# Folding four-by-four block weights into gate and key matrices: TensorE transposes and matmuls, or elementwise products on VectorE

## The chip, the cores and the metric

The kernel runs on one core of a Trainium2 chip. The metric is the device time of one execution in microseconds (us), lower is better. The core has TensorE (PE, matmuls, with its weight loads shown as PEld), VectorE (DVE), ScalarE (ACT), GpSimd (POOL), and SyncE (SP), which issues most DMAs.

## What is computed

The reference runs two transformer-like blocks on one sequence of 1024 positions and 1024 features. The change touches the mLSTM branch of the first block, cut here to what matters:

```python
QKV_BLOCK = 4          # w_q, w_k, w_v: (256, 4, 4); D_MLSTM = 1024
def headwise(u, w):    # block-diagonal linear map
    return jnp.einsum('bsni,nio->bsno', u.reshape(B, S, w.shape[0], w.shape[1]), w).reshape(B, S, -1)
...
    c = jax.nn.silu(centred_depthwise_conv(u, conv_w, conv_b))
    q = headwise(c, w_q)
    k = headwise(c, w_k)
    v = headwise(u, w_v)
    qkv = jnp.concatenate([q, k, v], axis=-1).astype(jnp.float32)
    gates = jnp.einsum('bsc,ncg->nbsg', qkv, w_gates.astype(jnp.float32)) \
        + b_gates.astype(jnp.float32)[:, None, None, :]
```

The kernel does not form q, k and v for the gates. It folds each block-diagonal map into the gate weights: gates = c (Wq Gq + Wk Gk) + u (Wv Gv), where G is `w_gates` (2 directions, 3072 rows, 8 columns). For the attention-like scores q k it folds likewise: with A = Wk Wq^T / 16 it needs only c and c A.

## The kernel before

Everything is fp32. A large projection is done as three matmuls of 512 columns on split operands (high and low parts, tiles `whi`, `wlo` of the weights and `u_hi`, `u_lo` of the activations; lines 829 to 831). A "group" is 24 such matmuls (8 pieces of the contraction times 3) into one PSUM bank, or 12 for the output projections. Weights come in chunks of 1 MB: SyncE loads chunk w into `wraw` once chunk w-1 has been split (`wt`, lines 391 and 394), and GpSimd splits it (`split`: a cast to `whi`, L610, a subtraction to `wlo`, L612).

The stages around the change, in the order in which TensorE meets them:

1. Output projection of the pool branch: chunks `W_OP` to `W_OP + 3`, eight 12-matmul groups each, in quarters q = 0 to 3. For each group VectorE adds the PSUM bank to `hst` (L1418), 32 additions in all. Quarters 0 and 1 fill one half of the features, 2 and 3 the other. Quarter 0 uses eight banks, the later ones take turns on four. SyncE loads `hst` (L453), stores finished parts (`hpool`, L457) and reloads, in an order written out by hand.
2. Projection `W_MX` to `W_MX + 3`, four groups each. ScalarE copies each group to `um` (L2020). VectorE runs the five-tap convolution over `um`, eight tiles `cva` (L1429, L1433), ScalarE's silu writes `cc` (L2008).
3. After each of the chunks `W_MX + 1` to `W_MX + 3`: GpSimd has expanded one of w_q, w_k, w_v (tile `wn`) to eight block-diagonal 128x128 tiles `bd` (L638), TensorE transposes the eight (L956), ScalarE copies them to `bt` (L2013).
4. Projection `W_MZ` to `W_MZ + 3`, four groups each; ScalarE writes `mzs` (L2036). After the second group of `W_MZ` TensorE multiplies `bt` by the gate weights `wg` (L967 for q and k, L970 for v; 16 columns each) and `bt` by `bt` (L976, eight of 128 columns). ScalarE copies the results to `ga` (L2040) and `Amat` (L2044).
5. After the fourth group of `W_MZ`: the gate sums, 32 matmuls of `ga` with `cc` and `um` (L986), then a reduction (L995), and from there a chain of row operations that ends before the recurrent units start. Heads 0 to 3 follow, with `Amat` applied in `headwise` (L1026).

The places that a sentence can't say:

```python
            for n in range(3):
                for i in range(4):
                    group(W_MX + n + 1, i, u_hi, u_lo, "a_um", 4 * n + 4 + i + 1)
                for b in range(2):
                    ps = ring_x("a_bt", 2 * n + b + 1)
                    for i in range(4):
                        pe.wait_ge(s["g_bd"], KT * n + 4 * b + i + 1)
                        mm = pe.transpose(ps[:, i * P:(i + 1) * P], bd[:, 4 * b + i, :], idn)
```

## Time and profile before

| what | value |
|---|---|
| median of 3 timed runs | 1254.55 us (1253.87 to 1254.64) |
| the profiled execution's own time | 1250.48 us |
| its span, first to last instruction | 1248.6 us |
| PE / PEld / DVE / ACT / POOL busy | 1208.9 / 966.7 / 660.4 / 349.6 / 469.4 us |
| mean granted TensorE clock | 0.990 of full speed |

The span is what the trace covers; times in the rows are us from its start. Busy time is the union of an engine's instructions. The trace was taken in one execution, whose own time is 4.07 us under the median of the timed runs. DMA queue rows (SPq) show the issue of a transfer, not its flight.

### The profile page before, as it was taken

Reading aid. Unit: us, or ns where it says so; the run is one execution under the profiler, and the core shown is the slowest. Engines: PE = TensorE matmul, PEld = TensorE weight load, DVE = VectorE, ACT = ScalarE, POOL = GpSimd, SP = SyncE. Lnnn points to the kernel's source line nnn. Section 1 sums busy time; section 2 is a strip of 40 time slices with the busy share of each in tenths; the row PEclk is TensorE's granted clock in tenths of the full one; section 3 lists DMA queues with packets and bytes.
Section 4 is the critical chain, followed back from the end, with each engine's and each line's share of the span. In section 5 each row is a group of like instructions: output and inputs, shape, how many; then the busy total and the mean of one; then the engine's idle time right before and its main releaser. Section 6 shows DMA issues by size and latency. Waiting matters only on the chain.

```text
span 1248.6 us, 15984 instructions
## 1 busy us (share of the span) xinstructions
PE 1208.9 (97%) x5977; PEld 966.7 (77%) x5977; DVE 660.4 (53%) x1220; ACT 349.6 (28%) x710; POOL 469.4 (38%) x449
## 2 busy tenths in 40 slices
PE   6999999999999999999998999889999999999995
PEld 5777878788888878787786788779888886667784
DVE  4325355422465203167767946856694525445468
ACT  6211110100022112446565421321111144433211
POOL 3224222232545223444665654314322324443343
PEclk9999999999999999999999999989999999999998
DMA  6131121243311223100114412222121110051112
GB/s 216 56 131 43 36 75 34 101 169 101 75 49 53 68 68 106 60 26 24 54 39 144 166 46 70 83 97 69 51 68 35 59 35 35 5 190 34 37 50 118
DMA packets 72702, 92.84 MB, mean 74 GB/s; under 512 B 12721, under 2 KB 51849, under 8 KB 72114
## 3 DMA queue, kind: packets, MB, share of 16 engines
q1 hardware_dynamic: 63906, 87.62, 21.0%
q10 hardware_dynamic: 8720, 4.20, 1.2%
q8 instruction: 49, 0.80, 0.3%
q14 instruction: 27, 0.22, 0.1%
HBM read 74.45 MB, written 18.92 MB: 75 GB/s over the span
## 4 chain that ended last, share of the span: by engine, by line
PE 88%; DVE 6%; POOL 2%; DMA 1%; issue 1%; ACT 1%; SPq 0%; ACTq 0%; POOLq 0%; DVEq 0%
PE bank L829 22%; PE bank L831 21%; PE bank L830 21%; PE bank L1078 3%; PE bank L1095 3%; PE wide L1251 2%; PE wide L930 2%; PE bank L1232 2%; PE wide L1241 2%; PE wide L1088 2%; DVE res L1908 1%; DMA wraw<-in_w_in 1%; PE bank L1038 1%; PE bank L1049 1%; PE bank L1026 1%
## 5 line engine op out<-in xcount | busy, mean ns | idle before, releaser
L610 POOL CAST whi<-wraw 128x2048 fp32r<-128x2048 f32 x32 | 60.6, 1894 | 448.9 <-PE bank L831 361.1
L829 PE MATMUL bank<-u_hi,wlo 128*128 128x512 f32 x512 | 202.7, 396 | 2.9 <-DVE u_lo L1349 2.9
L831 PE MATMUL bank<-u_hi,whi 128*128 128x512 f32 x512 | 200.1, 391 | 0.0
L830 PE MATMUL bank<-u_lo,whi 128*128 128x512 f32 x512 | 199.9, 390 | 0.0
L612 POOL TENSOR_TENSOR wlo<-wraw,whi 128x2048 fp32r<-128x2048 f32 x33 | 155.9, 4725 | 3.1 <-ACT whi L2230 0.5
L829 PE MATMUL bank<-x_hi,wlo 128*128 128x512 f32 x320 | 129.2, 404 | 7.2 <-POOL wlo L612 6.4
L830 PE MATMUL bank<-x_lo,whi 128*128 128x512 f32 x320 | 125.5, 392 | 0.0
L831 PE MATMUL bank<-x_hi,whi 128*128 128x512 f32 x320 | 125.5, 392 | 0.0
L829 PEld LDWEIGHTS bank<-u_hi,wlo 128*128 128x128 f32 x512 | 96.6, 189 | 25.9 <-DVE u_lo L1349 4.0
L831 PEld LDWEIGHTS bank<-u_hi,whi 128*128 128x128 f32 x512 | 96.5, 188 | 20.4
L830 PEld LDWEIGHTS bank<-u_lo,whi 128*128 128x128 f32 x512 | 96.5, 188 | 20.2 <-issue 0.7
L829 PEld LDWEIGHTS bank<-x_hi,wlo 128*128 128x128 f32 x320 | 60.6, 189 | 28.8 <-issue 9.8
L775 POOL TENSOR_SCALAR sp<-sp,rcx 128x384 f32<-128x384 f32 (+1 forms) x64 | 36.0, 575 | 112.3 <-DVE rcx L1840 112.3
L831 PEld LDWEIGHTS bank<-x_hi,whi 128*128 128x128 f32 x320 | 60.6, 189 | 13.1
L830 PEld LDWEIGHTS bank<-x_lo,whi 128*128 128x128 f32 x320 | 60.7, 190 | 11.6
L1753 DVE SCALAR_TENSOR_TENSOR wide<-glu,VT,wide 128x1024 f32<-128x1024 f32 x58 | 69.3, 1283 | 0.0
L1095 PE MATMUL bank<-v,kwb 128*128 128x257 f32 x224 | 58.2, 383 | 1.1 <-DVE Cst L1556 0.9
L1078 PE MATMUL bank<-Cst,qT 128*128 128x257 f32 x224 | 58.1, 381 | 0.9 <-ACT tmpj L2149 0.8
L2020 ACT ACTIVATE um<-bank 128x512 f32<-128x512 f32 x16 | 9.6, 599 | 157.2 <-PE bank L831 157.2
L698 POOL TENSOR_TENSOR Pm<-ST,Wb 128x128 f32<-128x128 f32 x64 | 30.4, 475 | 59.0 <-ACT Wb L2101 59.0
L829 PE MATMUL bank<-whi,ym_lo 128*128 128x512 f32 x128 | 50.2, 392 | 0.2 <-ACT tmpj L2149 0.2
L1834 DVE CUSTOM_DVE_ANT_0 sp<-bank,rbias,nsink 128x384 f32<-128x384 f32 (+1 forms) x64 | 34.9, 583 | 29.4 <-PE bank L1232 29.1
(330 smaller groups left out, 2430.7 us busy)
## 6 DMA issues: line engine op xcount, KB each, us to landing
wraw<-in_w_in SPq DMA_DIRECT2D x27, 1024.0 KB, 5.4
wraw<-in_w_out SPq DMA_DIRECT2D x12, 1024.0 KB, 5.1
xr<-in_x SPq DMA_DIRECT2D x8, 512.0 KB, 8.7
hst<-in_x SPq DMA_DIRECT2D x4, 1024.0 KB, 6.0
hpool<-hst SPq DMA_DIRECT2D x4, 1024.0 KB, 4.1
smz<-mzs SPq DMA_DIRECT2D x16, 256.0 KB, 2.1
wraw<-nmax ACTq DMA_DIRECT2D x32, 128.0 KB, 3.0
h<-hpool SPq DMA_DIRECT2D x4, 1024.0 KB, 6.8
```

What stands on the lines that cost most here:

```text
L610: g_.tensor_copy(whi[w % 2][:, :, :], wraw[:, :, :]).then_inc(s["w_hi"], 1)
L612: g_.tensor_tensor(wlo[w % 2][:, :, :], wraw[:, :, :], whi[w % 2][:, :, :].bitcast(F32), ALU.subtract).then_inc(s["w_lo"], 1)
L698: g_.tensor_tensor(Pm[:, n % 2, :], STs[h % 2][:, ck, :], Wb[:, n % 2, :], ALU.mult).then_inc(s["g_P"], 1)
L775: g_.tensor_scalar(row, row, rcx[:, x % 2, i:i + 1], 0.5 if g else 1.0, ALU.mult, ALU.mult).then_inc(s["g_nm"], 1)
L829: pe.matmul(ps, al, bh, start=(k == 0), stop=False)
L830: pe.matmul(ps, ah, bl, start=False, stop=False)
L831: return pe.matmul(ps, ah, bh, start=False, stop=(k == nk - 1))
L930: mm = pe.matmul(ps[:, :], pw[:, g % 2, k, dt * P:(dt + 1) * P], px[:, k, PAD + nh * HALF:PAD + (nh + 1) * HALF], start=(k == 0), stop=(k ...
L1078: mm = pe.matmul(ps[:, 0:AUG], q[:, k, ck * P:(ck + 1) * P], Cst[:, d, k, :], start=(k == 0), stop=(k == 1))
L1095: mm = pe.matmul(ps[:, 0:AUG], kwb[:, m % 2, k * P:(k + 1) * P], v[:, ck, :], start=True, stop=True)
L1753: ins = ve.scalar_tensor_tensor(dst, src, w, acc, ALU.mult, ALU.add)
L1834: ve.tensor_tensor_reduce(sp[:, x % 2, i, BAND - nb * P:BAND], ps[:, 0:nb * P], rbias[:, 2 * p + i, off:off + nb * P], 1.0, nsink[:, h:h + 1],
```

## The change

The products with the four-by-four blocks are no longer made on TensorE. The gate weights are loaded in another arrangement, four neighbouring rows of `w_gates` per partition, the same in four partitions (`wgx`, partitions i, i+4, ...; eight DMAs of 32 partitions), and so is `w_k` (`wkx`, four DMAs). VectorE then multiplies `wgx` by `wn`, with each of its four columns spread over eight gates (two products of 128x768), sums over the four (two reductions), and adds the q and k parts or copies the v part straight into `ga`; `fold_keys` makes the four-by-four blocks of A (`ak`) in the same way, and GpSimd expands `ak` to `Amat`. These eight steps stand on VectorE one ahead of each addition of quarter 2 of the pool output projection. The DMAs stand on SyncE right behind the load of `W_OP + 2`. The 24 transposes, the 32 small matmuls, `bd`, `bt`, `wg` and the nine ScalarE copies go. The gate sums wait for `v_ga` and `g_init`; the first use of `Amat` waits for `g_am`. The ring of banks 4 to 7 (`ring_x`) is taken nine times fewer, so later takers get another bank than before.

The core of the diff (names of tiles and semaphores left out):

```diff
@@ -227,7 +227,7 @@
-         cva, mzs, bd, bt, wg, ga,
+         cva, mzs, _m, wgx, gx, gr, ga, wkx, kx, ak,
-            [("cva", [P, 2, S], F32), ("mzs", [P, 2, HALF], F32), ("bd", [P, KT, P], F32),
-             ("bt", [P, 3, KT, P], F32), ("wg", [P, 24, 2, 8], F32), ("ga", [P, 16, 32], F32)],
+            [("cva", [P, 2, S], F32), ("mzs", [P, 2, HALF], F32), ("_m", [P, KT, P], F32),
+             ("wgx", [P, 2, 24, 4, 8], F32), ("gx", [P, 2, 24, 4, 8], F32), ("gr", [P, 2, 24, 8], F32),
+             ("ga", [P, 16, 32], F32), ("wkx", [P, KT, 4, 4], F32), ("kx", [P, KT, 4, 4], F32),
+             ("ak", [P, KT, 4], F32)],
...
@@ -459,6 +461,13 @@
             for q in range(2):
                 load_h(0, q)
             wt(W_OP + 2)
+            for i in range(4):
+                for d in range(2):
+                    sp_.dma_start(wgx[i::4, d, :, :, :],
+                                  I["w_gates"][0, d].rearrange("(c b o) g -> b c o g", b=32, o=4)
+                                  ).then_inc(s["l_wg"], 16)
+                sp_.dma_start(wkx[i::4, :, :, :], I["w_k"][0].rearrange("(j b) i o -> b j i o", b=32)
+                              ).then_inc(s["l_wg"], 16)
             for q in range(2):
                 store_h(0, q)
                 sp_.wait_ge(s[f"o_h{q}"], 16)
@@ -469,9 +478,6 @@
                 store_h(1, q)
             for q in range(2):
                 sp_.wait_ge(s[f"o_h{q}"], 32)
-            for d in range(2):
-                sp_.dma_start(wg[:, :, d, :], I["w_gates"][0, d].rearrange("(c p) g -> p c g", p=P)
-                              ).then_inc(s["l_wg"], 16)
             for w in range(W_OP + 6, W_MZ + 2):
                 wt(w)
 
@@ -629,20 +635,20 @@
 
             g_.wait_ge(s["l_wn"], 48)
             g_.wait_ge(s["l_cst"], 16)
+            g_.wait_ge(s["v_ylo"], 16)
+            g_.memset(ga[:, :, 16:32], 0.0).then_inc(s["g_init"], 1)
+            g_.wait_ge(s["v_ga"], 7)
             g_.wait_ge(s["o_h0"], 32)
             g_.wait_ge(s["o_h1"], 32)
-            g_.memset(ga[:, :, 16:32], 0.0).then_inc(s["g_init"], 1)
             blk = cst[:, C_BLK:C_BLK + 32].unsqueeze(2).to_broadcast([P, 32, 4])
 
-            def expand(dst, n, j):
+            def expand(dst, four):
                 return g_.tensor_tensor(dst.rearrange("p (b o) -> p b o", o=4),
-                                        wn[:, n, j, :].unsqueeze(1).to_broadcast([P, 32, 4]), blk, ALU.mult)
-
+                                        four.unsqueeze(1).to_broadcast([P, 32, 4]), blk, ALU.mult)
+
+            for j in range(KT):
+                expand(Amat[:, j, :], ak[:, j, :]).then_inc(s["g_am"], 1)
             for n in range(3):
-                if n:
-                    g_.wait_ge(s["t_bt"], 2 * n)
-                for j in range(KT):
-                    expand(bd[:, j, :], n, j).then_inc(s["g_bd"], 1)
                 split(W_MX + 2 + n)
...
-                    expand(bdh[:, m, :], 2, 2 * h + m).then_inc(s["g_bdh"], 1)
+                    expand(bdh[:, m, :], wn[:, 2, 2 * h + m, :]).then_inc(s["g_bdh"], 1)
...
@@ -949,47 +955,23 @@
             for n in range(3):
                 for i in range(4):
                     group(W_MX + n + 1, i, u_hi, u_lo, "a_um", 4 * n + 4 + i + 1)
-                for b in range(2):
-                    ps = ring_x("a_bt", 2 * n + b + 1)
-                    for i in range(4):
-                        pe.wait_ge(s["g_bd"], KT * n + 4 * b + i + 1)
-                        mm = pe.transpose(ps[:, i * P:(i + 1) * P], bd[:, 4 * b + i, :], idn)
-                    mm.then_inc(s["t_bt"], 1)
-
             for i in range(4):
                 group(W_MZ, i, u_hi, u_lo, "a_mz", i + 1)
-                if i == 1:
-                    pe.wait_ge(s["a_bt"], 6)
-                    pe.wait_ge(s["l_wg"], 32)
-                    ps = ring_x("a_bt", 7)
-                    for j in range(KT):
-                        for n in range(2):
-                            pe.matmul(ps[:, j * 16:j * 16 + 16], bt[:, n, j, :], wg[:, KT * n + j, :, :],
-                                      start=(n == 0), stop=(n == 1))
-                    for j in range(KT):
-                        mm = pe.matmul(ps[:, (KT + j) * 16:(KT + j) * 16 + 16], bt[:, 2, j, :],
-                                       wg[:, 2 * KT + j, :, :], start=True, stop=True)
-                    mm.then_inc(s["t_bt"], 1)
-                    for b in range(2):
-                        ps = ring_x("a_bt", 8 + b)
-                        for k in range(4):
-                            mm = pe.matmul(ps[:, k * P:(k + 1) * P], bt[:, 0, 4 * b + k, :], bt[:, 1, 4 * b + k, :],
-                                           start=True, stop=True)
-                        mm.then_inc(s["t_bt"], 1)
-            pe.wait_ge(s["a_bt"], 7)
+            pe.wait_ge(s["v_ga"], 6)
+            pe.wait_ge(s["g_init"], 6)
             pe.wait_ge(s["a_c"], KT)
             for nh in range(2):
-                ps = ring_x("a_bt", 10 + nh)
+                ps = ring_x("a_gsum", nh + 1)
                 for j in range(16):
                     q = 32 * (j % 4)
                     src = cc if j < KT else um
                     mm = pe.matmul(ps[q:q + 32, :], ga[:, j, :], src[:, j % KT, nh * HALF:(nh + 1) * HALF],
                                    start=(j < 4), stop=(j >= 12))
-                mm.then_inc(s["t_bt"], 1)
+                mm.then_inc(s["t_gsum"], 1)
             for i in range(4):
                 group(W_MZ + 1, i, u_hi, u_lo, "a_mz", 4 + i + 1)
                 if i == 1:
-                    pe.wait_ge(s["a_bt"], 11)
+                    pe.wait_ge(s["a_gsum"], 2)
                     ps = ring_x("v_gs", 4)
                     for t in range(NT):
                         mm = pe.matmul(ps[:, t * 16:t * 16 + 16], gsum[:, t * P:(t + 1) * P],
@@ -1022,6 +1004,8 @@
                 n, i = i // 4, i % 4
                 if n == 0:
                     m, nh = i // 2, i % 2
+                    if h == 0 and i == 0:
+                        pe.wait_ge(s["g_am"], KT)
                     ps = fill("a_hq", 12 * h + i + 1)
                     mm = pe.matmul(ps[:, :], Amat[:, 2 * h + m, :], cc[:, 2 * h + m, nh * HALF:(nh + 1) * HALF],
                                    start=True, stop=True)
@@ -1407,9 +1391,45 @@
                                          ).then_inc(s["v_ylo"], 1)
                         ve.wait_ge(s["v_ylo"], n + 1)
 
+            def fold_gates(step):
+
+                if step < 2:
+                    if step == 0:
+                        ve.wait_ge(s["l_wn"], 48)
+                        ve.wait_ge(s["l_wg"], 16 * 12)
+                    w = wn[:, :, :, :].rearrange("p n j o -> p (n j o)").unsqueeze(2).to_broadcast([P, 96, 8])
+                    ins = ve.tensor_tensor(gx[:, step, :, :, :].rearrange("p c o g -> p (c o) g"),
+                                           wgx[:, step, :, :, :].rearrange("p c o g -> p (c o) g"), w, ALU.mult)
+                elif step < 4:
+                    ve.wait_ge(s["v_ga"], step - 1)
+                    ins = ve.tensor_reduce(gr[:, step - 2, :, :],
+                                           gx[:, step - 2, :, :, :].rearrange("p c o g -> p c g o"), AX_X, ALU.add)
+                elif step == 4:
+                    ve.wait_ge(s["v_ga"], 4)
+                    ins = ve.tensor_tensor(ga[:, 0:KT, 0:16].rearrange("p j (d g) -> p d j g", d=2),
+                                           gr[:, :, 0:KT, :], gr[:, :, KT:2 * KT, :], ALU.add)
+                else:
+                    ins = ve.tensor_copy(ga[:, KT:2 * KT, 0:16].rearrange("p j (d g) -> p d j g", d=2),
+                                         gr[:, :, 2 * KT:3 * KT, :])
+                ins.then_inc(s["v_ga"], 1)
+
+            def fold_keys(step):
+
+                if step == 0:
+                    wq = wn[:, 0, :, :].unsqueeze(2).to_broadcast([P, KT, 4, 4])
+                    chain(ve.tensor_tensor(kx[:, :, :, :], wkx[:, :, :, :], wq, ALU.mult))
+                else:
+                    chain(ve.tensor_reduce(ak[:, :, :], kx[:, :, :, :], AX_X, ALU.add))
+                    ve.tensor_scalar(ak[:, :, :], ak[:, :, :], HD ** -0.5, None, ALU.mult).then_inc(s["v_ga"], 1)
+
             for q in range(4):
                 for t in range(NT):
                     n = 8 * q + t
+                    if q == 2:
+                        if t < 6:
+                            fold_gates(t)
+                        else:
+                            fold_keys(t - 6)
                     if q % 2:
                         ve.wait_ge(s["v_hp"], n - 7)
                     else:
@@ -2007,12 +2027,6 @@
                 ac.wait_ge(s["v_conv"], j + 1)
                 ac.activation(cc[:, j, :], cva[:, j % 2, :], ACT.Silu).then_inc(s["a_c"], 1)
 
-            def bt_copy(n):
-                for b in range(2):
-                    ps = filled(ac, "t_bt", 2 * n + b + 1, "a_bt", 2 * n + b + 1)
-                    ac.activation(bt[:, n, 4 * b:4 * b + 4, :], ps[:, :].rearrange("p (j c) -> p j c", j=4), ACT.Copy
-                                  ).then_inc(s["a_bt"], 1)
-
             for h in range(NH):
                 for i in range(4):
                     m, nh = i // 2, i % 2
@@ -2023,8 +2037,6 @@
                         conv_silu(2 * h - 2)
                     if h and i == 3:
                         conv_silu(2 * h - 1)
-                if h:
-                    bt_copy(h - 1)
             conv_silu(6)
             for n in range(16):
                 h, m, nh = n // 4, n % 4 // 2, n % 2
@@ -2034,19 +2046,10 @@
                 if n >= 2:
                     ac.wait_ge(s[f"o_mz{n % 2}"], 16 * (n // 2))
                 ac.activation(mzs[:, n % 2, :], ps[:, :], ACT.Silu).then_inc(s["a_mz"], 1)
-                if n == 1:
-                    ps = filled(ac, "t_bt", 7, "a_bt", 7)
-                    ac.wait_ge(s["g_init"], 6)
-                    ac.activation(ga[:, :, 0:16], ps[:, 0:2 * P].rearrange("p (j g) -> p j g", j=16), ACT.Copy
-                                  ).then_inc(s["a_bt"], 1)
-                    for b in range(2):
-                        ps = filled(ac, "t_bt", 8 + b, "a_bt", 8 + b)
-                        ac.activation(Amat[:, 4 * b:4 * b + 4, :], ps[:, :].rearrange("p (j c) -> p j c", j=4),
-                                      ACT.Copy, scale=HD ** -0.5).then_inc(s["a_bt"], 1)
                 if n == 3:
                     for nh in range(2):
-                        ps = filled(ac, "t_bt", 10 + nh, "a_bt", 10 + nh)
-                        ac.activation(gsum[:, nh * HALF:(nh + 1) * HALF], ps[:, :], ACT.Copy).then_inc(s["a_bt"], 1)
+                        ps = filled(ac, "t_gsum", nh + 1, "a_gsum", nh + 1)
+                        ac.activation(gsum[:, nh * HALF:(nh + 1) * HALF], ps[:, :], ACT.Copy).then_inc(s["a_gsum"], 1)
                 if n == 9:
 
                     ac.wait_ge(s["v_rif"], 2)
```

Where the instructions stand, engine by engine. Operand names are tiles of the program (`wide` and `bank` are PSUM), "waits" lists semaphores, xN is N alike in a row. TensorE before, after the second group of `W_MZ`:

```order
L831 MATMUL bank<-u_hi,whi 128x512
L967 MATMUL wide<-wg,bt 128x16 [waits a_bt,l_wg]
L967 MATMUL wide<-wg,bt 128x16 x15
L970 MATMUL wide<-wg,bt 128x16 x8
L976 MATMUL wide<-bt 128x128 [waits a_bt]
L976 MATMUL wide<-bt 128x128 x3
L829 MATMUL bank<-u_hi,wlo 128x512 [waits a_um,w_lo]
```

TensorE now, from the end of the fourth group of `W_MZ` (the second group runs straight into the third):

```order
L837 MATMUL bank<-u_hi,whi 128x512
L968 MATMUL wide<-cc,ga 32x512 [waits a_c,v_hp,g_init,v_ga]
L968 MATMUL wide<-cc,ga 32x512 x7
L968 MATMUL wide<-um,ga 32x512 x8
L968 MATMUL wide<-cc,ga 32x512 [waits v_hp]
L835 MATMUL bank<-u_hi,wlo 128x512 [waits a_mz,w_lo]
```

The small matmuls are gone, and the gate sums (L986 before) are now L968, the first that waits for the fold. SyncE now, from the load of `W_OP + 2`:

```order
L393 DMA wraw<-in_w_out 128x4x512 [waits w_lo]
L466 DMA wgx<-in_w_gates 32x24x32 x2
L469 DMA wkx<-in_w_k 32x8x16
...
L459 DMA hpool<-hst 128x4x512 [waits v_hp]
L455 DMA hst<-in_x 128x4x512 [waits o_h0]
L393 DMA wraw<-in_w_out 128x4x512 [waits w_lo]
```

The three lines L466, L466, L469 come four times, twelve DMAs, where there was none between `wraw` and `hpool`; the two of `wg` that stood before the load of `W_OP + 6` are gone. VectorE now, from the first addition of quarter 2:

```order
L1438 TENSOR_TENSOR hst<-bank,hst 128x512 [waits t_gemm,v_hp] x8
L1401 TENSOR_TENSOR gx<-wgx,wn 128x768 [waits l_wg,l_wn]
L1438 TENSOR_TENSOR hst<-bank,hst 128x512 [waits t_gemm,l_xh0]
L1401 TENSOR_TENSOR gx<-wgx,wn 128x768
L1438 TENSOR_TENSOR hst<-bank,hst 128x512 [waits t_gemm,l_xh0]
L1405 TENSOR_REDUCE gr<-gx 128x192 [waits v_ga]
...
L1409 TENSOR_TENSOR ga<-gr 128x2x8x8 [waits v_ga]
...
L1422 TENSOR_REDUCE ak<-kx 128x32
L1423 TENSOR_SCALAR ak<-ak 128x32 [waits v_chain]
```

Before, these were additions alone (L1418); each now has one or two small instructions ahead of it.

## Rows read from the trace of the kernel before

**Rows 1.** The page's first part: engine, busy us, share of the span, instructions.

```profile
PE 1208.9 (97%) x5977; PEld 966.7 (77%) x5977; DVE 660.4 (53%) x1220; ACT 349.6 (28%) x710; POOL 469.4 (38%) x449
```

**Rows 2.** The page's chain that ended last, by engine.

```profile
PE 88%; DVE 6%; POOL 2%; DMA 1%; issue 1%; ACT 1%; SPq 0%; ACTq 0%; POOLq 0%; DVEq 0%
```

**Rows 3.** Timeline of ACT: start us, us, line, operation, idle before and its releaser.

```profile
356.89 0.60 ACT L2020 ACTIVATE um<-bank 128x512 f32<-128x512 f32 x1 [4.85 <-PE bank L831]
363.25 0.60 ACT L2020 ACTIVATE um<-bank 128x512 f32<-128x512 f32 x1 [3.84 <-PE bank L831]
...
402.26 0.60 ACT L2020 ACTIVATE um<-bank 128x512 f32<-128x512 f32 x1 [4.85 <-PE bank L831]
...
408.62 0.60 ACT L2036 ACTIVATE mzs<-bank 128x512 f32<-128x512 f32 x1 [2.89 <-PE bank L831]
414.36 1.06 ACT L2008 ACTIVATE cc<-cva 128x1024 f32<-128x1024 f32 x1 [5.14 <-DVE cva L1433]
...
428.30 0.60 ACT L2036 ACTIVATE mzs<-bank 128x512 f32<-128x512 f32 x1 [4.87 <-PE bank L831]
433.74 0.60 ACT L2036 ACTIVATE mzs<-bank 128x512 f32<-128x512 f32 x1 [4.84 <-PE bank L831]
```

**Rows 4.** Windows: stretch, length, then busy us of each engine, granted clock, DMA share, GB/s.

```profile
413.80:419.00 5.20, 5.20 (x48) 5.16 (x48) 0.52 (x1) 1.54 (x2) 0.00 (x0) 1.00 0.24 86
419.00:422.50 3.50, 3.50 (x20) 3.50 (x19) 0.00 (x0) 0.98 (x2) 0.00 (x0) 0.53 0.00 0
...
433.60:440.60 7.00, 7.00 (x65) 1.98 (x64) 0.00 (x0) 1.19 (x2) 6.45 (x2) 1.00 0.10 37
```

**Rows 5.** Groups of PE instructions in 413.8 to 422.6: busy us, mean ns, idle before.

```profile
L976 PE MATMUL wide<-bt 128*128 128x128 f32 x16 | 3.7, 423 | 0.0
L967 PE MATMUL wide<-wg,bt 128*128 128x16 f32 x32 | 3.6, 260 | 0.0
L970 PE MATMUL wide<-wg,bt 128*128 128x16 f32 x16 | 1.9, 263 | 0.0
```

**Rows 6.** Timeline of DVE, the additions at the start of quarter 2.

```profile
272.63 0.69 DVE L1418 TENSOR_TENSOR hst<-bank,hst 128x512 f32<-128x512 f32 x1 [2.03 <-PE bank L831]
275.35 0.69 DVE L1418 TENSOR_TENSOR hst<-bank,hst 128x512 f32<-128x512 f32 x1 [2.03 <-PE bank L831]
```

**Rows 7.** Timeline of SP, issues of DMAs during stage 1.

```profile
231.16 0.51 SPq L391 DMA_DIRECT2D wraw<-in_w_out  x1
259.75 0.37 SPq L457 DMA_DIRECT2D hpool<-hst  x1
263.91 0.37 SPq L453 DMA_DIRECT2D hst<-in_x  x1
264.32 1.27 SPq L391 DMA_DIRECT2D wraw<-in_w_out  x1
```

**Rows 8.** Lines 424 and 473 on SP: issue ns min/median/max, first and last start us; landing.

```profile
L424 SPq DMA_DIRECT2D wn<-in_w_k x1: 2645/2645/2645, 14.2 to 14.2; - x1
...
L473 SPq DMA_DIRECT2D wg<-in_w_gates x2: 373/1558/2742, 318.4 to 318.8; - x2
...
DMA to landing us min/median/max: 4.0/5.0/6.1
```

**Rows 9.** Timeline of POOL: the splits in stage 1 and at 337 us.

```profile
273.31 1.90 POOL L610 CAST whi<-wraw 128x2048 fp32r<-128x2048 f32 x1 [18.55 <-DMA wraw<-in_w_out]
275.29 4.62 POOL L612 TENSOR_TENSOR wlo<-wraw,whi 128x2048 fp32r<-128x2048 f32 x1
...
337.19 4.93 POOL L612 TENSOR_TENSOR wlo<-wraw,whi 128x2048 fp32r<-128x2048 f32 x1
```

**Rows 10.** Timeline of DVE, convolution: one instruction, and four of the next tile.

```profile
337.70 5.50 DVE L1433 SCALAR_TENSOR_TENSOR cva<-um,VT,cva 128x1022 f32<-128x1022 f32 x1
...
348.50 5.24 DVE L1433 SCALAR_TENSOR_TENSOR cva<-um,VT,cva 128x1022 f32<-128x1022 f32 x4
```

**Rows 11.** Windows, as Rows 4: a stretch with TensorE idle.

```profile
810.00:820.00 10.00, 6.03 (x17) 4.80 (x18) 9.74 (x11) 1.49 (x2) 5.06 (x4) 0.66 0.13 52
```

8 lines of the change are left out of this document (4 added, 4 removed).

## The prediction

> **What bounds the kernel now.** I read the page first. TensorE is busy for 1208.9 of the 1248.6 us of the span [rows 1], and the chain of waits that ended last lies on TensorE for 88% [rows 2]. So an instruction taken off TensorE shortens the run by its own time, unless TensorE then waits for something else. An instruction added to VectorE (busy for 53%) costs nothing as long as it fits into that engine's gaps. The rest of the reading answers two questions: how long the removed TensorE work takes, and whether each thing that TensorE will now wait for is ready in time.
>
> For the first I went to ScalarE's timeline, not to the matmul durations: matmuls overlap, but ScalarE takes each group's bank as soon as the group ends, so the distances between its copies are the true pace of TensorE [rows 3]. A group without extras takes 5.44 us (428.30 to 433.74).
>
> **What goes from TensorE.** One block of eight transposes lies between the copies at 356.89 and 363.25: 6.36 us in place of 5.44, so 0.92 us [rows 3]. The third block reads the same (402.26 to 408.62, 6.36). Three blocks: **2.75 us**. The small matmuls (L967, L970, L976) stand behind the second group of `W_MZ`. Its own copy was held up on ScalarE by the silu at 414.36, so I count from the first group's copy: 408.62 to the third group's at 428.30 is 19.68 us for two groups (10.88) and the block. The block costs **8.80 us** [rows 3]. The instructions' own times agree: 3.6, 1.9 and 3.7 us [rows 5]. Sum: **11.55 us**, and nothing is added to TensorE, only waits.
>
> **The clock inside that block.** TensorE had no idle time from 413.80 to 419.00, at full clock (2.4 GHz), yet from 419.00 to 422.50 the granted clock is 0.53, that is nearly all at the lower level, 1.2 GHz [rows 4]. Work of 16-column matmuls came before the fall. Of the 8.80 us, 3.50 x (1 - 0.53) = 1.6 us are this slow stretch, and they leave with the block. The Trainium skill ("TensorE: Matmul & The Clock Gate", "What's actually happening") says that the half rate is the default and comes back after idleness. That rule and the row disagree here: the engine was busy all through. By the rule alone the block would have run at full clock, and the sum would be 1.6 us less; the trace has the fall, so I keep 8.80.
>
> **What is added to SyncE and the DMA queues.** Twelve DMAs are issued behind the load at 231.16 (issued by 231.67), and the next one in the old order is the store at 259.75 [rows 7]: 28.1 us of room. No row shows a DMA of this shape. The nearest are the gate weights' and key weights' own loads, many small pieces too: 0.37 to 2.74 us to issue, landing in 4.0 to 6.1 us [rows 8]. Twelve issues take 4.4 us at the lower end. At the upper end, 32.9 us, SyncE is free at 264.6, so 4.8 us late for the store. I take the middle of the range, 12 x 1.56 = 18.7 us, since it comes from the load of the same tensor, and it costs nothing. At the upper end the store, the reload at 263.91 and the weight load at 264.32 all slip by 4.8 us. The additions of quarter 2 start at 272.63 and today wait for TensorE, not for the reload [rows 6], so they slip by 4.8 us at most. GpSimd's split of the late chunk (273.31 to 279.91 [rows 9]) would end at 284.7. TensorE needs it for the first group of quarter 3. Additions come every 2.72 us [rows 6], so that group starts 7 x 2.72 = 19.0 us after 272.63, at 291.7. Hidden. The two `wg` issues that go had their own room and are worth nothing.
>
> **What is added to VectorE.** An addition of 512 columns takes 0.69 us and is followed by 2.03 us of waiting for TensorE [rows 6]. By columns a fold product of 768 takes 1.04 us; I give each of the two reductions the same, with twice that as the upper bound since it reads with a stride. The five small instructions are under 0.69 us each. That is at most 4 x 1.04 + 5 x 0.69 = 7.6 us in eight gaps that hold 16.2. What if one is late? TensorE has four banks, so an addition may slip by three groups less its own time, 8.16 - 0.69 = **7.5 us**, before TensorE stalls. There is one hazard. A convolution step issued at 337.70 took 5.50 us where four together take 5.24, and ended a microsecond after GpSimd's subtraction of 337.19 to 342.12 [rows 9, 10]: both read two tensors in SBUF. The second fold product comes at 273.3, in the middle of a split. If it waits for its end at 279.91, the next addition starts at 281.0 and not 275.35, 5.6 us late, still inside 7.5. Cost: nothing. The Trainium skill ("SBUF — State Buffer", "SBUF: two separate sides") speaks against such a placing: VectorE instructions with two SBUF inputs and GpSimd hold a shared port pair for a whole instruction, and the other blocks. The rows agree (5.50 us against 1.31). If every two-input fold met a full subtraction, lateness would add up past the slack; that is in the second rival.
>
> **What moves elsewhere.** GpSimd has 16 fewer expansions and no wait for TensorE's transposes, and its eight `Amat` expansions stand where eight `bd` ones stood. ScalarE loses nine copies. None was what TensorE waited for: nothing. The gate sums now stand 11.55 us earlier, at 422.1 in place of 433.6 [rows 4], and wait for the last silu. It ended at 414.36 + 1.06 = 415.4 [rows 3]. Even if it did not move, 6.7 us are left, and one more blocked convolution step (5.50 - 1.31 = 4.2 us) fits into that. Everything behind (row operations, heads, the second block) is released by TensorE's results and moves along.
>
> **The sum.** The profiled execution took 1250.48 us and should take 1238.9 (span 1237.1). The timed median is 1254.55, 4.07 above it; the same 11.55 us gives **1243.0 us**. A measurement of this kernel tells about 0.2%, 2.5 us, from no change.
>
> **The rivals.**
> - *The clock falls elsewhere* (chance 0.08). The fall follows the work around it and may reappear beside the gate sums, or in a stretch where TensorE idles, as at 810 to 820 with 0.66 [rows 11]. For it: matmuls run almost without a pause into the gate sums. Against: in 433.60 to 440.60 they ran at a granted clock of 1.00 [rows 4], and they are 512 columns wide. Price: one such stretch, 1.6 us, up to two: 1244.6 to 1246.2. The Trainium skill ("TensorE: Matmul & The Clock Gate", same section) calls the monitor free-running, so such falls need not stay with a place.
> - *VectorE's cover breaks* (0.07). Slow issues make the additions 4.8 us late; the second product is then issued at 278.1 beside a split of 278.1 to 284.7 and ends at 285.7, 10.4 us late. TensorE stalls for 10.4 - 7.5 = 2.9 us: 1245.9. Against: it needs both upper ends.
> - *Slower: the twelve copies land one behind the other* (0.04). The first product waits for all twelve, and every addition queues behind it. At 6.1 us each they are in at 231.7 + 73.2 = 304.9; with the product the addition starts at 305.9, 33.3 us late, TensorE stalls for 25.8, net +14.3: 1268.8. It decides from 4.9 us per copy (lateness 19.05 = 7.5 + 11.55). Against: today's loads overlap, and two of 96 KB each landed in 4.0 and 6.1 us [rows 8].
> - *The gate sums wait for the convolution* (0.02): two more blocked steps, 8.4 us against 6.7, and partly given back: 1244.7.
> - *No change* (0.03): the 11.55 us come back as waits of TensorE in the later stages that VectorE and GpSimd share in the chain (8% [rows 2]). For it: that share. Against: they start from TensorE's output and move along. 1254.5.
>
> **How the numbers follow.** The forecast has 0.76, and its own range is 1241 to 1245 (two microseconds either way for pauses that shift in later stages and for the spread of the runs). The clock and the broken cover take the range up to 1247; downward 1240.3, if the clock also loses less in a later idle stretch. The slower case and no change stay outside. Faster by over 0.2%: 0.76 + 0.08 + 0.07 + 0.02 = 0.93; within: 0.03; slower: 0.04.
>
> **What would show it.** Right: ScalarE's copies at 5.44 us from group to group from the first of `W_MX` to the fourth of `W_MZ`; the gate sums near 422 with no idle time before them; the granted clock 1.00 there; the small VectorE instructions at about 1 us in the gaps of quarter 2, the additions every 2.72 us; the store at 259.75 unmoved; the stretch from the gate sums to the end as long as before. Wrong: TensorE idle between 275 and 300 with VectorE as releaser, a row of `gx` released by a DMA, an idle time before the gate sums, or a later stage that has grown by microseconds.

## The result and the profile after

| | before | after |
|---|---|---|
| median of the timed runs, same chip | 1254.21 us (4 runs, 1252.36 to 1254.64) | 1239.2 us (4 runs, 1237.97 to 1240.01) |
| ratio, with 95% interval | | 0.9882 [0.9865, 0.9899] |
| profiled execution, own time | 1250.48 us | 1238.44 us |
| its span | 1248.6 us | 1236.4 us |
| mean granted clock | 0.990 | 0.992 |

The change is faster, by 1.2%. The forecast was 1243.0 us with a range of 1240.3 to 1247.0. The time lies 1.1 us below that range. The gain was 15.0 us (the ratio gives 14.8), against 11.55 forecast. Between the two *profiled* executions it is 12.04 us: 1238.44 us was measured where the sum gave 1238.9. So the sum nearly holds for the profiled pair and not for the timed medians. That is the hint: something differed between the profiled execution of before and the ones that were timed. One of the 91 executions of the kernel before in all comparisons took 1528.84 us at a granted clock of 0.751, and it is left out everywhere below.

The page's first part after the change, to be held against [rows 1]:

```profile
PE 1196.0 (97%) x5889; PEld 953.8 (77%) x5889; DVE 673.2 (54%) x1229; ACT 345.2 (28%) x701; POOL 456.5 (37%) x433
```

TensorE has 88 instructions and 12.9 us less, and is as full as before. VectorE has nine more (a net 12.8 us, of which the fold's own are 6.8; most of the rest is in the convolution, see below), ScalarE nine fewer (the copies), GpSimd sixteen fewer (the expansions).

ScalarE's timeline, the copies that pace TensorE, to be held against [rows 3]:

```profile
360.40 0.60 ACT L2034 ACTIVATE um<-bank 128x512 f32<-128x512 f32 x1 [3.89 <-PE bank L837]
365.84 0.60 ACT L2034 ACTIVATE um<-bank 128x512 f32<-128x512 f32 x1 [4.84 <-PE bank L837]
...
403.92 0.60 ACT L2048 ACTIVATE mzs<-bank 128x512 f32<-128x512 f32 x1 [2.95 <-PE bank L837]
410.55 1.06 ACT L2028 ACTIVATE cc<-cva 128x1024 f32<-128x1024 f32 x1 [6.04 <-DVE cva L1453]
...
414.80 0.60 ACT L2048 ACTIVATE mzs<-bank 128x512 f32<-128x512 f32 x1 [2.70 <-PE bank L837]
420.24 0.60 ACT L2048 ACTIVATE mzs<-bank 128x512 f32<-128x512 f32 x1 [4.84 <-PE bank L837]
```

Every distance is now 5.44 us: 360.40 to 365.84, and 403.92 to 414.80 is two groups, 10.88. The transposes and the small matmuls have left without a trace, and 428.30 has become 414.80. The last silu ends at 410.55 + 1.06 = 411.6.

TensorE's timeline at the gate sums, and below it the windows of that stretch (columns as in [rows 4]):

```profile
419.81 0.39 PE L837 MATMUL bank<-u_hi,whi 128*128 128x512 f32 x1
420.13 1.92 PE L968 MATMUL wide<-cc,ga 128*32 128x512 f32 x16
```

```profile
413.80:419.00 5.20, 5.20 (x25) 4.30 (x24) 0.00 (x0) 0.60 (x1) 0.00 (x0) 1.00 0.13 50
...
420.20:427.20 7.00, 7.00 (x65) 1.97 (x65) 0.00 (x0) 1.20 (x2) 6.46 (x2) 1.00 0.11 40
```

No idle time stands before the gate sums, at 420.1 us, and the clock is 1.00 all through. They have 420.1 - 411.6 = 8.5 us in hand against the silu that they wait for.

VectorE's timeline of the convolution shows one more thing that moved. One tile (four steps), before and after:

```profile
359.51 5.32 DVE L1433 SCALAR_TENSOR_TENSOR cva<-um,VT,cva 128x1022 f32<-128x1022 f32 x4
```

```profile
357.54 9.46 DVE L1453 SCALAR_TENSOR_TENSOR cva<-um,VT,cva 128x1022 f32<-128x1022 f32 x4
```

Before, two of the eight tiles held a step of 5.50 us beside a GpSimd subtraction; now four do. These are the two more blocked steps that the prediction's fourth rival asks for, 8.4 us in sum. They fell into different tiles, in time that VectorE had to spare, and cost nothing: the last tile, with one blocked step, is as it was. The count is four in every trace with the fold, also where TensorE's work was put back (both_back below), so it goes with what changed on GpSimd and VectorE and not with TensorE's pace.

VectorE's timeline in quarter 2, where the fold stands in the gaps of [rows 6]:

```profile
267.99 0.69 DVE L1438 TENSOR_TENSOR hst<-bank,hst 128x512 f32<-128x512 f32 x1 [2.03 <-PE bank L837]
268.60 0.95 DVE L1401 TENSOR_TENSOR gx<-wgx,wn 128x768 f32<-128x768 f32 x1
270.71 0.69 DVE L1438 TENSOR_TENSOR hst<-bank,hst 128x512 f32<-128x512 f32 x1 [1.16 <-PE bank L837]
271.32 1.43 DVE L1401 TENSOR_TENSOR gx<-wgx,wn 128x768 f32<-128x768 f32 x1
273.43 0.69 DVE L1438 TENSOR_TENSOR hst<-bank,hst 128x512 f32<-128x512 f32 x1 [0.68 <-PE bank L837]
274.04 1.59 DVE L1405 TENSOR_REDUCE gr<-gx 128x192 f32<-128x768 f32 x1
276.15 0.69 DVE L1438 TENSOR_TENSOR hst<-bank,hst 128x512 f32<-128x512 f32 x1 [0.52 <-PE bank L837]
```

The additions still come every 2.72 us and still wait for TensorE; only their idle time has shrunk, from 2.03 to 0.52 us at the least. That is how a hidden cost looks. The fold of the keys behind them is small (0.28, 0.28 and 0.18 us). The hazard of the prediction, a product held up to the end of a split, did not come: the second product ran into a GpSimd cast (270.04 to 271.94) and took 1.43 us in place of 0.95, and both reductions took 1.59 us beside the subtraction that started at 272.01.

SyncE's timeline, to be held against [rows 7]:

```profile
229.79 3.97 SPq L466 DMA_DIRECT2D wgx<-in_w_gates  x2
...
243.89 0.65 SPq L469 DMA_DIRECT2D wkx<-in_w_k  x1
257.83 0.38 SPq L459 DMA_DIRECT2D hpool<-hst  x1
```

The twelve issues run from 229.79 to 244.5 and the store still stands 1.9 us ahead of 259.75, the shift that the whole trace has there: SyncE had been idle for 13 us. Nothing landed later than 9.5 us after its issue, and so at least 15 us before the product at 268.60.

Laid on top of each other, instruction by instruction, the two traces differ by -1.9 us from the first 20 us on (start-up, granted clock 0.66 in 15 to 20 us before, 1.00 after), three times -0.9 at the transposes, -8.8 at the block, +1.9 at the first unit of the recurrence, and -0.6 at a stall near 810 us: -12.2. So the sum of 11.55 us is there to a tenth, and two other things of 1.9 us each cancelled, which is luck. The start-up goes with the execution and not with the kernel: a second trace of the changed kernel (after_again) has 0.69 in 15 to 20 us, and from there on stands 1.4 us behind the first. The loss at the first unit does go with the kernel. It is the prediction's first rival, "The clock falls elsewhere", which had a chance of 0.08 and a price of 1.6 us.

### The profile page after: what moved, and what is told of

Its sections match the earlier page's. It is cut to its first block, busy times and chain, and to the rows that moved or that the text cites. A ratio compares the mean times of both kernels' runs of the same rounds, so it can differ in the third digit from the quotient of the medians.

```text
span 1236.4 us, 15797 instructions
## 1 busy us (share of the span) xinstructions
PE 1196.0 (97%) x5889; PEld 953.8 (77%) x5889; DVE 673.2 (54%) x1229; ACT 345.2 (28%) x701; POOL 456.5 (37%) x433
## 4 chain that ended last, share of the span: by engine, by line
PE 87%; DVE 6%; POOL 2%; DMA 1%; issue 1%; ACT 1%; SPq 0%; ACTq 0%; POOLq 0%; DVEq 0%
PE bank L835 22%; PE bank L837 21%; PE bank L836 21%; PE bank L1062 3%; PE bank L1079 3%; PE wide L1235 2%; PE wide L936 2%; PE bank L1216 2%; PE wide L1225 2%; PE wide L1072 2%; DVE res L1928 1%; DMA wraw<-in_w_in 1%; PE bank L1022 1%; PE bank L1033 1%; PE bank L1010 1%
## 5 line engine op out<-in xcount | busy, mean ns | idle before, releaser
L1453 DVE SCALAR_TENSOR_TENSOR cva<-um,VT,cva 128x1022 f32<-128x1022 f32 (+1 forms) x32 | 58.0, 1811 | 1.1
```

The source lines that it names most:

```text
L1453: ins = ve.scalar_tensor_tensor(acc[:, a0:a1], um[:, j, a0 + sh:a1 + sh], tap(q), acc[:, a0:a1], ALU.mult, ALU.add)
```

## The experiments

Three theories were to be told apart; the expectations below name them by number. Theory 1: the 3.5 us of gain over the forecast are chance, of few runs and of the clock at start-up or elsewhere. Theory 2: the block of small matmuls costs more in most executions than the 8.80 us of the first trace. Theory 3: something other than TensorE's own work was saved too (ScalarE, GpSimd, the waits that went).

Several of these kernels add matmuls whose results nobody reads.

**1. Both kernels again.** No edit.

> The kernel before once more, unchanged, for its spread and a second trace. Theory 1 (chance of the clock): ratio to before 0.998 to 1.002, runs between 1250 and 1255 us, and where this trace differs from the first one it differs by steps of about 1 to 2 us that stand at a lower granted clock (the start-up stretch of 15 to 20 us in the first one, or the first units). Theory 2 (the small matmuls catch more of the lower clock in most executions than in the first trace): the block of small matmuls takes more than 8.8 us here, up to 12. Theory 3 (something else than TensorE's own work differs): same time, and no such steps.

> The changed kernel once more. Theory 1: over more runs the gain comes towards 11.6 us plus or minus 2, ratio 0.989 to 0.992, and the trace again has the block of 11.55 us gone and nothing else but steps at a lower granted clock. Theory 2: the ratio stays at 0.988 or lower. Theory 3: the ratio stays at 0.988 and no step in the trace stands at a lower clock.

Measured: before_again 1252.17 us (12 runs), ratio 1.0009 [0.9997, 1.0021]; after_again 1240.07 us (6 runs), ratio 0.9919 [0.9903, 0.9935]. The kernel before had 29 runs there, median 1250.57, and they spread from 1248.39 to 1254.89. The four of the first comparison (1252.36 to 1254.64) lie in the upper half of that spread. So after_again fits theory 1: over more runs the gain comes down towards 11.6 us.

The trace of before_again shows why such a spread exists. ScalarE's timeline of it, then the windows over the block (columns as in [rows 4]):

```profile
408.40 0.60 ACT L2036 ACTIVATE mzs<-bank 128x512 f32<-128x512 f32 x1 [2.86 <-PE bank L831]
...
431.33 0.60 ACT L2036 ACTIVATE mzs<-bank 128x512 f32<-128x512 f32 x1 [6.03 <-PE bank L831]
```

```profile
413.00:416.00 3.00, 3.00 (x26) 2.88 (x25) 1.12 (x1) 1.54 (x2) 0.00 (x0) 1.00 0.39 137
416.00:419.00 3.00, 3.00 (x20) 3.00 (x19) 0.00 (x0) 0.00 (x0) 0.00 (x0) 0.62 0.23 87
419.00:422.00 3.00, 3.00 (x15) 3.00 (x16) 0.00 (x0) 0.38 (x1) 0.00 (x0) 0.50 0.00 0
422.00:425.00 3.00, 3.00 (x15) 2.90 (x15) 0.00 (x0) 0.89 (x2) 0.00 (x0) 0.50 0.00 0
425.00:428.00 3.00, 3.00 (x11) 2.36 (x10) 0.00 (x0) 0.30 (x1) 0.00 (x0) 0.67 0.00 0
```

431.33 - 408.40 = 22.93 us for two groups (10.88) and the block: **12.05 us**, where the first trace had 8.80 [rows 3]. The instructions are the same, and TensorE is busy in every microsecond. The granted clock is low from 416 to past 425 us, and not for 3.5 us as in [rows 4]. The time lost to it, 3 x (0.38 + 0.50 + 0.50 + 0.33) = 5.1 us, leaves 6.9 us of block at full clock; the first trace gives 8.80 - 1.6 = 7.2. The slow stretch even reaches into the 512-column group behind the block. The two profiled executions took 1250.48 and 1254.01 us: 3.25 of those 3.53 us are the block. That is theory 2, in one execution.

The runs without a trace bear this out as far as they can, since each has its mean granted clock on record. Of 86 executions of the kernel before in the three later comparisons, the 13 quickest (up to 1249.2 us) all have 0.992, and the 17 slowest (from 1253.4 us) have 0.986 to 0.988. The spread goes with the clock; where in the run the clock was low, only a trace tells.

**2. The removed TensorE work put back, unused.** Into the changed kernel, behind the second group of `W_MZ`, 32 small matmuls of the same sizes (64 instructions in the profile; small_back); and in both_back also the three blocks of transposes:

```diff
             for i in range(4):
                 group(W_MZ, i, u_hi, u_lo, "a_mz", i + 1)
+                if i == 1:
+                    pe.wait_ge(s["v_ga"], 6)
+                    pe.wait_ge(s["g_am"], KT)
+                    ps = ring_x("v_ga", 6)
+                    for j in range(KT):
+                        for n in range(2):
+                            pe.matmul(ps[:, j * 16:j * 16 + 16], Amat[:, j, :], ga[:, j, 0:16],
+                                      start=(n == 0), stop=(n == 1))
...
```

> The changed kernel with only the small matmuls put back as dead work behind the second group of W_MZ (24 of 16 columns, 8 of 128). Theory 1: 8.8 us over the changed kernel, 7.1 if the clock stays up through the block; ratio to before about 0.997. Theory 2: 11 to 12 us over the changed kernel in the timed runs, ratio to before 0.998 to 1.000, and the block in the trace stands at the lower clock for most of its length. Theory 3: 8.8 us over the changed kernel, ratio to before 0.995.

> The changed kernel with all the removed TensorE work put back as dead work at its old places (24 transposes, 24 matmuls of 16 columns, 8 of 128; their results are read by nobody), the fold still on VectorE. Theory 1 and theory 2: as slow as before, 0.999 to 1.001 of it, since TensorE's work was all that the change took away. Theory 3 (the rest of the gain comes from ScalarE, GpSimd or the waits that went): 0.997 to 0.998, 3 us faster than before.

Measured: small_back 1250.95 us (12 runs), ratio 1.0000 [0.9987, 1.0014], so 10.9 us over after_again of the same comparison. both_back 1252.98 us (12 runs), ratio 1.0014 [1.0002, 1.0026], 12.9 us over after_again. So TensorE's own work is the whole gain: with VectorE's fold, the twelve DMAs and the moved waits all in place, putting the work back brings the old time back. Theory 3 expected both_back 3 us faster than before and is refuted; it is even 1.8 us slower, by an interval that leaves out 1 (the last section has a candidate). And small_back, with 10.9 us, comes near the 11 to 12 us of theory 2 and not the 8.8 of the others. The price of the block is again not fixed. In small_back the copies stand at 405.54 and 426.86, a block of 21.32 - 10.88 = 10.44 us; in both_back at 408.35 and 428.03, 8.80 us. The windows of small_back show the low clock inside the block:

```profile
413.00:416.00 3.00, 3.00 (x25) 3.00 (x24) 0.00 (x0) 0.71 (x2) 0.00 (x0) 0.83 0.24 90
416.00:419.00 3.00, 3.00 (x15) 3.00 (x15) 0.00 (x0) 0.00 (x0) 0.00 (x0) 0.50 0.00 0
419.00:422.00 3.00, 3.00 (x13) 2.71 (x12) 0.00 (x0) 0.00 (x0) 0.00 (x0) 0.53 0.00 0
422.00:425.00 3.00, 3.00 (x15) 2.44 (x14) 0.00 (x0) 0.00 (x0) 0.00 (x0) 1.00 0.00 0
```

**3. Only the transposes put back.** The edit adds, behind each four groups of `W_MX`, two banks of four transposes of `Amat`, read by nobody.

> The changed kernel with the 24 transposes alone put back as dead work at their three old places. Theory 1 (the transposes cost their own time, 0.92 us a block, and the clock stays up through them): 2.75 us over the changed kernel, granted clock 1.00 around each block, ratio to before about 0.993. Rival (they too bring the clock down, or they let waits of TensorE go): more than 4 us over the changed kernel.

Measured: 1243.45 us (6 runs), ratio 0.9943 [0.9926, 0.996]. ScalarE's timeline of this kernel:

```profile
355.33 0.60 ACT L2039 ACTIVATE um<-bank 128x512 f32<-128x512 f32 x1 [4.85 <-PE bank L837]
361.66 0.60 ACT L2039 ACTIVATE um<-bank 128x512 f32<-128x512 f32 x1 [4.78 <-PE bank L837]
367.10 0.60 ACT L2039 ACTIVATE um<-bank 128x512 f32<-128x512 f32 x1 [4.84 <-PE bank L837]
```

6.33 - 5.44 = 0.89 us per block, three times, at a granted clock of 1.00. The 2.75 us of the forecast hold, and these matmuls of 128 columns bring no fall. The median stands 3.6 us over that of all runs of the changed kernel (1239.84, 15 runs); with six runs and this spread (1241.32 to 1247.24) the 0.9 us between the two are not told apart from chance.

**4. The small matmuls split.** In the kernel before, the 24 matmuls of 16 columns stand behind the first group of `W_MZ`, the eight of 128 columns behind the second:

```diff
-                if i == 1:
+                if i == 0:
                     pe.wait_ge(s["a_bt"], 6)
...
+                if i == 1:
                     for b in range(2):
                         ps = ring_x("a_bt", 8 + b)
```

> The kernel before with its small matmuls in two portions: the 24 of 16 columns behind the first group of W_MZ, the 8 of 128 behind the second, so that 5.44 us of wide matmuls lie between. Theory 1 (the long unbroken stretch of narrow matmuls brings the clock down, and what it costs swings from 8.8 to 12.05 us with the execution): the two portions together cost 7.1 to 7.5 us with the clock at 1.00, 1.5 to 5 us less than before, ratio 0.997 to 0.999, and a smaller spread. Rival (any short stretch of narrow matmuls brings it down, or the fall has nothing to do with them): the fall is there after the first portion, ratio 1.000 or above.

Measured: 1252.47 us (12 runs), ratio 1.0007 [0.9997, 1.0017]: no gain from splitting. The theory had expected 1.5 to 5 us, with the clock up; its rival holds. The windows show the fall in the 16-column matmuls again, and it moved with them: it starts two windows (6 us) earlier than in before_again:

```profile
407.00:410.00 3.00, 3.00 (x29) 3.00 (x28) 2.93 (x3) 0.25 (x1) 0.30 (x1) 1.00 0.57 155
410.00:413.00 3.00, 3.00 (x16) 3.00 (x15) 2.31 (x2) 0.00 (x0) 0.00 (x0) 0.51 0.81 282
413.00:416.00 3.00, 3.00 (x10) 2.42 (x10) 0.00 (x0) 1.33 (x2) 0.00 (x0) 0.50 0.00 0
416.00:419.00 3.00, 3.00 (x13) 2.41 (x12) 0.00 (x0) 0.00 (x0) 0.00 (x0) 0.86 0.00 0
```

So the fall goes with the 16-column matmuls, at both places where they stood, and goes on through 512-column matmuls of the next group. Only the eight of 128 columns were moved away from them; a finer split was not tried. The copies stand at 406.66 and 427.98: 10.44 us for both pieces, of which the second, at full clock, is 427.98 - 420.74 - 5.44 = 1.80.

**5. VectorE's cover tried to its limit.** All eight steps of the fold ahead of the first addition of quarter 2, in place of one per gap:

```diff
-                    if q == 2:
-                        if t < 6:
-                            fold_gates(t)
-                        else:
-                            fold_keys(t - 6)
+                    if q == 2 and t == 0:
+                        for step in range(8):
+                            if step < 6:
+                                fold_gates(step)
+                            else:
+                                fold_keys(step - 6)
```

> The changed kernel with all eight VectorE steps (some 7 us) in a lump ahead of the first addition of quarter 2. Theory (an addition may slip by 7.5 us before TensorE stalls): the first addition is 6 to 7 us late, TensorE has no idle time there or under 0.5 us, the additions have caught up within four; time as the changed kernel within 0.1%. Rival (VectorE and GpSimd block each other in the split that falls there, so the lump takes over 8 us): TensorE idles 1 to 5 us between 270 and 290, time longer by as much.

Measured: 1241.07 us (6 runs), ratio 0.9918 [0.9903, 0.9933]. VectorE's timeline, then GpSimd's:

```profile
270.56 0.69 DVE L1439 TENSOR_TENSOR hst<-bank,hst 128x512 f32<-128x512 f32 x1 [2.03 <-PE bank L837]
271.17 1.82 DVE L1401 TENSOR_TENSOR gx<-wgx,wn 128x768 f32<-128x768 f32 x2
272.91 3.10 DVE L1405 TENSOR_REDUCE gr<-gx 128x192 f32<-128x768 f32 x2
...
276.39 4.70 DVE L1420 TENSOR_TENSOR kx<-wkx,wn 128x128 f32<-128x128 f32 x1
...
281.54 2.48 DVE L1439 TENSOR_TENSOR hst<-bank,hst 128x512 f32<-128x512 f32 x4
285.44 0.69 DVE L1439 TENSOR_TENSOR hst<-bank,hst 128x512 f32<-128x512 f32 x1 [1.43 <-PE bank L837]
```

```profile
276.25 4.69 POOL L618 TENSOR_TENSOR wlo<-wraw,whi 128x2048 fp32r<-128x2048 f32 x1
```

The first addition should have started 2.72 us behind 270.56, at 273.3, and started at 281.54: 8.3 us late. TensorE's one answer, in its waits:

```profile
PE bank L835 <- DVE hst L1439: 1.0, 1, 1.0
```

1.0 us of stall from 8.3 us of lateness: the slack of the four banks is 7.3 us, against 7.5 argued. Four additions in a row bring VectorE back in step: before the fifth it again waits for TensorE, 1.43 us. This is the rival that the cover breaks, made true by force, and it costs a microsecond in the trace; the median is 1.2 us over the changed kernel's, which six runs do not tell from nothing. And the 128-column product, 0.28 us in the changed kernel, took 4.70 us: issued 0.14 us after GpSimd's subtraction began, it ended when that ended (281.09 and 280.94). The Trainium skill ("SBUF — State Buffer", "SBUF: two separate sides") says that a VectorE instruction with two SBUF inputs and a GpSimd one that reads SBUF lock each other out for a whole instruction; the trace agrees, at 4.4 us for this one.

**6. The low clock elsewhere taken away.** The changed kernel still had low clock at the first unit of the recurrence and behind the stall on `wlo` near 800 us. In warm, two unused 512-column matmuls stand before the first unit's wait, and 24 before the group that ends the stall:

```diff
+                    ps = take(4 + n % 4, "v_h", n + 1)
+                    if n == 0:
+                        for _ in range(2):
+                            pe.matmul(ps[:, :], Amat[:, 0, :], cc[:, 0, 0:HALF], start=True, stop=True)
                     pe.wait_ge(s["g_P"], n + 1)
-                    ps = take(4 + n % 4, "v_h", n + 1)
...
+                ps = ring_g("a_glu", n)
+                if (w, i) == (1, 0):
+                    for _ in range(24):
+                        pe.matmul(ps[:, :], x2_hi[:, 0, 0:P], x2_hi[:, 0, 0:HALF], start=True, stop=True)
+                group(W_2 + w, i, x2_hi, x2_lo, "a_glu", n, ps=ps)
```

> The changed kernel with dead wide matmuls in two pauses of TensorE: 2 of 512 columns fp32 while it waits for the first recurrent unit (2.0 us of idle time at 509), 24 of 512 columns (5.4 us) while it waits 6.4 us for the split of the second chunk of w_in_2 at 796. Theory (the granted clock falls because of the thin stretches there and costs 1.3 to 1.9 us each time): both falls gone, 2 to 4 us faster than the changed kernel, ratio to before 0.987 to 0.989. Rival (the falls come from elsewhere or only move): the same time as the changed kernel, or slower by what the dead matmuls hold up (under 1 us).

Measured: 1236.6 us (4 runs), ratio 0.9884 [0.9869, 0.9900], as the theory expected; the clock stays at 1.00 in both places.

**7. The same in parts, and both kernels a third time.** warm_unit has the first of the two additions, warm_stall the second.

> The kernel before once more, for a third comparison of two equal programs and one more trace of its block of small matmuls. Ratio to the kernel before 1.000 (0.998 to 1.002). Theory (the block has no one price, since the granted clock falls in it for a varying time): the block costs something between 8 and 12.5 us again, by the two copies of mzs around it less 10.88 us, with low clock inside it; a rival (its price is the 8.80 of the first trace, and the 12.05 of the second was a disturbance) expects 8.7 to 9.0. The start of the recurrence, at about 525 us, is at full clock as in both traces before, if the fold has to do with the fall there; if that fall is chance, it may show here.

> The changed kernel once more. If the first comparison (0.9882 with 4 runs) was lucky in its few runs, as the second (0.9919) suggests, the ratio is 0.990 to 0.993 (1238.5 to 1242 us). If the chip decides between the two, it may be 0.988 again. Trace: the fall of the granted clock at the first unit of the recurrence (about 512 us) is there again if it goes with the fold; six traces of kernels with the fold showed it and three without did not.

> The changed kernel with only the two unused matmuls of 512 columns between the last work before the recurrence and its first unit, nothing in the later stall. The fall at about 512 us goes; by the two traces it cost 1.2 to 1.9 us, so against the changed kernel of the same call -1 to -2 us, ratio 0.001 to 0.0015 lower. Rival: the gain of the kernel with both additions came from the stall at about 800 us alone, then this one equals the changed kernel and the low clock is gone at no profit.

> The changed kernel with only the 24 unused matmuls in the stall on wlo, at about 800 us. The low clock of some 7 us behind the stall goes; PE has 0.5 to 3 us of idle time inside that stretch anyway, so -1.5 to -2.5 us against the changed kernel of the same call. Rival: what comes behind the stall is bound by VectorE's wlo products, and a higher clock there only lengthens the next waits: then -0.5 us or less. The sum of the two parts should be the 3.5 us of the kernel with both (ratio 0.9884 against 0.9919, from two calls).

Measured, all on one chip, with 17 runs of the kernel before (median 1251.49 us):

| kernel | median | ratio [95%] |
|---|---|---|
| before_third | 1250.83 us | 0.9993 [0.9982, 1.0004] |
| after_third | 1239.78 us | 0.9906 [0.9892, 0.992] |
| warm_unit | 1239.46 us | 0.99 [0.9886, 0.9913] |
| warm_stall | 1238.52 us | 0.989 [0.9877, 0.9904] |

The block of before_third costs 431.46 - 408.55 - 10.88 = 12.03 us. The rival that 12.05 had been a disturbance falls: of three traces of the kernel before, two have 12.0. The prices seen, 8.80, 10.44 and 12.05, stand 1.6 us apart, as the low stretch gets longer.

The windows of after_third, then of warm_stall (the two stretches in question, columns as in [rows 4]):

```profile
508.00:512.00 4.00, 2.27 (x14) 1.26 (x12) 0.74 (x2) 1.94 (x6) 1.61 (x4) 0.97 0.46 131
512.00:516.00 4.00, 3.71 (x9) 2.67 (x10) 0.64 (x2) 0.78 (x2) 3.34 (x8) 0.60 0.12 32
798.00:802.00 4.00, 0.00 (x0) 0.00 (x0) 3.93 (x3) 0.46 (x2) 3.92 (x2) 0.99 0.00 0
802.00:806.00 4.00, 2.43 (x6) 1.95 (x7) 3.90 (x5) 0.00 (x0) 2.66 (x4) 0.50 0.15 59
806.00:810.00 4.00, 4.00 (x14) 3.13 (x13) 3.83 (x8) 1.49 (x2) 0.00 (x0) 0.66 0.20 76
```

```profile
798.00:802.00 4.00, 4.00 (x20) 3.30 (x19) 3.93 (x3) 0.58 (x2) 3.92 (x2) 1.00 0.00 0
802.00:806.00 4.00, 2.79 (x13) 1.98 (x12) 3.93 (x4) 0.00 (x0) 3.08 (x4) 1.00 0.04 15
806.00:810.00 4.00, 4.00 (x19) 3.33 (x18) 3.83 (x8) 1.70 (x3) 0.00 (x0) 1.00 0.28 116
```

The unused matmuls fill 798 to 802 us, in which TensorE stood still, and the clock stays at 1.00. Instruction by instruction, warm_stall is 2.1 us quicker across the stall than after_third (2.4 us behind the stall, less 0.3 because `wlo` came that much later), and warm_unit 1.4 us quicker across the first unit. In the medians the parts show as 1.3 and 0.3 us, which these runs do not tell from each other nor from the traces' 2.1 and 1.4. The kernel with both has the lowest median of all, 1236.6 us, 3.2 us under the 1239.84 of the changed kernel's 15 runs. Its interval [0.9869, 0.9900] lies wholly below that of after_again, but overlaps the lower end of after_third's and most of the first comparison's. All four of its executions (1235.09 to 1237.53) lie below the quickest of the changed kernel's 15 (1237.93). So it is probably the fastest version; the reservation is that the two did not run in one comparison, and that it has four runs.

## Why the prediction was right in its mechanism and wrong in its number

**Right.** TensorE bounds the kernel and work taken off it comes back as time: small_back and both_back show it by putting it back. Each block of transposes is 0.89 to 0.92 us. Twelve DMAs, nine VectorE instructions and the moved waits cost nothing in the stages where they stand; SyncE was busy for 14.7 us (18.7 assumed). The reductions took 1.59 us each, between the 1.04 assumed and its double. The banks' slack is 7.3 us where 7.5 was argued. The gate sums waited for nothing, though the two more blocked convolution steps of the fourth rival came. The slower rival (copies one behind the other) is refuted by landings of 2.1 to 9.5 us in which they overlapped. Against its profiled execution, the sum gave 1238.9 us and 1238.44 was measured, with the two terms of 1.9 us that cancelled by luck.

**The step that failed is "The block costs 8.80 us" together with "the trace has the fall, so I keep 8.80".** I read it from one execution, and it is one draw of a price that varies: 8.80, 12.05 and 12.03 us in three traces of the kernel before, 10.44 and 8.80 in two with the same matmuls put back, 10.44 where they were split. With the clock up it would be about 7 us, an estimate from 8.80 - 1.6 and 12.05 - 5.1; no run shows it. The execution profiled was one of the cheap ones. The text had the warning in hand: "The timed median is 1254.55, 4.07 above it; the same 11.55 us gives 1243.0". Those 4.07 us were taken as belonging to work that stays. By the trace of before_again, whose execution took 1254.01 us, 3.25 us of such a difference stand in the very block that the change removes. Priced by that trace, the change takes off 2.75 + 12.05 = 14.8 us, and 1254.55 becomes 1239.75; measured were 1239.2. The half microsecond flatters it: the sum leaves out the loss at the first unit. With 1.4 to 1.9 us for that it gives 1241.2 to 1241.7, and the last 2 us are not accounted for; they are within the spread of either kernel's runs. That the four timed runs of before had the dear block is argued and not shown: no trace of theirs exists, nor their clocks. The argument is their times, since in the other comparisons every execution as slow as three of them (1253.87 us or more) had a granted clock of 0.988 or less.

**A second step, smaller: "Everything behind (row operations, heads, the second block) is released by TensorE's results and moves along."** It did not quite: the first unit of the recurrence lost 1.9 us in the first pair of traces, and a fall of the clock stands there in all eight traces with the fold and no filled pause. The prediction had this only as a rival, at 0.08.

**The range** had no end for this. Its lower end, 1240.3, allowed 14.25 us of gain for other reasons, and the term of the block had no bounds at all, because it stood in a row. A price read at a clock that falls in the middle of it has two ends, here by estimate about 7 us with no fall and twice that with the low clock all through; 12.05 is the most that a trace shows.

**How much is the luck of runs.** Three of the four timed runs of before took 1253.87 us or more; of the other 86 executions, 11 did. The three comparisons gave 0.9882, 0.9919 and 0.9906. Over 90 runs of the kernel before on all chips, the median is 1251.5 us, and over 15 of the changed one 1239.84: 11.7 us. The forecast's gain of 11.55 fits that, but probably for a reason it did not know: on average a dearer block, and in return a slower first unit. How the executions of before divide between the cheap and the dear block can't be had from three traces, and stays open.

## What to carry to other kernels

A stretch with a lowered clock inside it has a price per execution, not one price. Take two or three traces before costing what is removed there, or carry both ends. If the timed median lies microseconds above the profiled execution, ask first which stretch could hold the difference, and whether the change touches it; taking it as a constant is a choice that has to be argued. And count the slack of the ring of banks before spreading work finely over another engine's gaps: with four banks and 2.72 us per group, an addition 8.3 us late cost 1.0 us here. Last, when work leaves one engine, look at where its other work then falls: here the splits met the convolution four times in place of two.
